# Loading two experts' down weights and the last gate's weights only after the first gathered rows, and turning the second rows between gate and up

## The reference, cut to what matters

```python
x = x + mix
x = x + hier_moe(rms_norm(x, norm2_g), ...)      # top-1 group of 4, top-2 experts of 4
x = x + sigmoid(x @ w_ple_gate) * (p @ w_ple)    # w_ple_gate is 1024 x 1024
y = rms_norm(x, final_norm_g)
# one expert e, for the rows that chose it:
act = silu(h @ w_gate[e]) * (h @ w_up[e]) * weight   # w_gate, w_up: 1024 x 256
out += act @ w_down[e]                               # w_down: 256 x 1024
```

## Time and profile before

| | us |
|---|---|
| timed runs, median of 3 | 892.86 |
| the profiled execution, own time | 888.35 |
| its span in the profile | 886.6 |
| TensorE busy | 851.8 (96%) |
| VectorE, ScalarE, GpSimd busy | 351.2, 201.5, 143.2 |
| mean granted TensorE clock | 0.991 |

### The profile page before, as it was taken

One profiled execution on the slowest core, in us unless ns is written; L12 is line 12 of the kernel. 1 busy time (PEld: TensorE's weight loads), 2 busy tenths in 40 slices (PEclk: granted clock), 3 DMA queues, 4 the chain that ended last, 5 costly groups with the idle time before them and its releaser, 6 DMA issues. The chain is left out here.

```text
span 886.6 us, 12016 instructions
## 1 busy us (share of the span) xinstructions
PE 851.8 (96%) x4227; PEld 580.2 (65%) x4227; DVE 351.2 (40%) x935; ACT 201.5 (23%) x495; POOL 143.2 (16%) x152
## 2 busy tenths in 40 slices
PE   8999999999999898989999999998999999999995
PEld 5455677777778696545677764454777777774441
DVE  3199702355542335667472451133311111114433
ACT  3010213311013164545321000231111111113121
POOL 3059002200003022345000000021111111003100
PEclk9999999999999899999999999999999999999998
DMA  9430875705113969000204292039799999965211
GB/s 334 112 102 0 187 256 154 64 1 182 40 38 93 126 186 283 9 1 1 108 1 111 81 333 76 6 124 335 251 348 368 375 362 363 359 221 190 75 48 35
DMA packets 110887, 140.47 MB, mean 158 GB/s; under 512 B 33910, under 2 KB 90298, under 8 KB 110722
## 3 DMA queue, kind: packets, MB, share of 16 engines
q1 hardware_dynamic: 93164, 110.17, 40.5%
q0 software_dynamic: 4304, 15.47, 5.2%
q10 hardware_dynamic: 13374, 14.22, 4.7%
HBM read 118.65 MB, written 23.29 MB: 160 GB/s over the span
## 5 line engine op out<-in xcount | busy, mean ns | idle before, releaser
L1062 PE MATMUL ps<-hT,w_slot 128*128 128x288 f32 x640 | 155.7, 406 | 0.2 <-ACT fin L1731 0.2
L1062 PEld LDWEIGHTS ps<-hT,w_slot 128*128 128x128 f32 x640 | 121.4, 190 | 34.3 <-issue 0.9
L1062 PE MATMUL ps<-w_slot,hT 128*128 128x512 f32 (+1 forms) x320 | 127.1, 555 | 1.9 <-DMA w_slot<-in_w_in 1.6
L1512 PE MATMUL ps<-wgu,hT 128*128 128x256 f32 x512 | 114.9, 383 | 0.7 <-DVE hT L1950 0.7
L1512 PEld LDWEIGHTS ps<-wgu,hT 128*128 128x128 f32 x512 | 98.3, 192 | 20.7 <-issue 6.7
L1062 PEld LDWEIGHTS ps<-w_slot,hT 128*128 128x128 f32 x320 | 60.0, 190 | 62.8 <-issue 42.4
L2395 DVE SCALAR_TENSOR_TENSOR th<-th,ps 128x256 f32<-128x256 f32 x16 | 6.7, 421 | 135.5 <-ACT th L1875 135.5
L1062 PE MATMUL ps<-merged,actT 128*128 128x512 f32 x128 | 58.8, 601 | 0.4 <-ACT actT L1879 0.4
L1062 PE MATMUL ps<-w_slot,merged 128*128 128x512 f32 x128 | 56.0, 594 | 1.1 <-DVE merged L1950 1.1
L1062 PEld LDWEIGHTS ps<-w_slot,merged 128*128 128x128 f32 x128 | 23.9, 190 | 29.9 <-issue 28.2
L1062 PEld LDWEIGHTS ps<-merged,actT 128*128 128x128 f32 x128 | 23.1, 189 | 24.7 <-issue 24.1
(11 more groups left out here) (402 smaller groups left out, 1153.8 us busy)
## 6 DMA issues: line engine op xcount, KB each, us to landing
wgu<-in_w_exp_gate SPq DMA_DIRECT2D x16, 1024.0 KB, 9.5
wgu<-in_w_exp_up SPq DMA_DIRECT2D x16, 1024.0 KB, 13.9
merged<-in_w_exp_down SPq DMA_DIRECT2D x16, 1024.0 KB, 12.5
w_slot<-in_w_in SPq DMA_DIRECT2D x8, 1024.0 KB, 7.3
expert_rows<-onsaT ACTq DMA_DIRECT2D x16, 512.0 KB, 6.8
hT<-gates_by_features SPq DMA_DIRECT2D x8, 576.0 KB, 3.8
w_slot<-in_w_o SPq DMA_DIRECT2D x2, 2048.0 KB, 9.1
w_slot<-in_w_ple_gate SPq DMA_DIRECT2D x2, 2048.0 KB, 24.4
```

The source lines that it names most:

```text
L1062: ins = pe.matmul(out, a, b, start=(n == 0), stop=(n == len(pairs) - 1))
L1512: ins = pe.matmul(ps[:, 2 + u, FF * w:FF * w + FF], hgT[:, u, k], wgu[:, u, w, k], start=(k == 0), stop=(k == KD - 1))
```

## The change

Two edits. SyncE waits for `hg_ld[1]`, the landing of expert 1's first gathered rows, before it issues the down weights of experts 0 and 1 and both halves of w_ple_gate. And TensorE does the turning of expert 1's rows between the gate half and the up half of gate_up(0), in place of behind gate_up(0).

```diff
             load_weights("ple")
             sp.wait_ge(pe_done, PLAN.done(("wo", NT - 2, 1)))
+            sp.wait_ge(hg_ld[1], 16)
             for u in range(2):
                 load_down(u, u)
             load_weights("pg0")
...
-            def gate_up(j, n, u, half):
+            def gate_up(j, n, u, half, between=None):
                 pe.wait_ge(gu_ld[u], j * 256 + half * 32 + 32)
                 for w in range(2):
+                    if w and between:
+                        between()
                     for k in range(KD):
...
-                gate_up(j, 0, 0, 0)
-                turn_rows(j, 1, 1, 0)
+                gate_up(j, 0, 0, 0, lambda: turn_rows(j, 1, 1, 0))
```

## The result

| | before | after |
|---|---|---|
| median of 22 timed runs of each, side by side (us) | 890.14 | 897.58 |
| fastest | 885.76 | 892.76 |
| ratio after / before, 95% interval | | 1.0085 [1.0056, 1.0113] |
| the profiled execution, span | 886.6 | 900.1 |

The change makes the kernel slower by 0.85%, some 7.6 us. The forecast was slower, by 3.85 us (0.43%): the way and the mechanism held, the size was half of what came.

A forecast was written before the change was run, and what follows sets the result against it. The prediction took TensorE to bound the expert stage, with DMA nearly as busy. Gate_up(2)'s start moves from 637.0 to 638.85, plus 2.0 us of clock: +3.85 on 892.86 gives 896.7 us, range 891.0 to 899.5.

The forecast's parts named there:

- Bound: Expert stage: TensorE is the chain, with DMA engines nearly as busy at 348 to 375 GB/s.
- The gather is freed: Ahead of gate_up(0): last store lands in 3.0 us, first gather starts 0.29 us after its list; 3.53 us halt gone.
- TensorE alone would be 6.0 us ahead at gate_up(2): Without waiting for weights, TensorE would reach gate_up(2) at 631.0 in place of 637.0.
- The backlog: Ahead of gate_up(2): SyncE released at 609.75, plus 18.4, 8.0 and 2.7 us; expert 2's weights land at 638.85.
- the worst bound: Latest landing of expert 2's weights, 641.3: release at 610, 371 GB/s ahead, 3.3 us for the rest.
- the 5 to 9 us named as a sign: Expected length of TensorE's halt ahead of gate_up(2) in the profile after, ended by the load of w_exp_up.
- the best bound: Earliest landing of expert 2's weights, 635.4: release at 608.25, all 9.96 MB at 400 GB/s, 2.2 us for the rest.
- The clock: In gate_up(2), after a halt of 7.9 us: half clock loses 2.0 us, bounds 0 and 3.
- Nothing late behind that: After gate_up(2): weight stream 1.3 us later, TensorE 3.85 later, so no second halt and the shift reaches the end.
- Bandwidth rule: Loads ahead of gate_up(2): at 358 GB/s the 7.34 MB take 20.5 us, time 898.8; prediction used 400 GB/s instead.
- The faster one: Rival, chance 0.10: expert 2's weights pass w_ple_gate at gate_up(2), TensorE keeps 6.0 us, time 886.9.
- slower by more: Rival, chance 0.13: landing at the worst bound, 641.3, or a second halt; +5.5 to +7 us, 898.4 to 900.

The follow-up runs named there:

- the kernels without the backlog: Kernel after with both halves of w_ple_gate issued behind the experts' last down load: ratio to before 0.9942 with SyncE's wait, 0.9931 without.
- nothing held: Kernel after without SyncE's wait, and with w_ple_gate's second half (pg1) issued behind the experts: ratio to before 0.9925.

## Why the prediction was right, and where its size was off

- *The number.* The absolute forecast, 896.7, lies 0.9 us from the 897.58 measured, and that is luck: it stands on a median of three runs, 892.86, where the median of 22 is 890.14. The shift is what the working gives, and it was +3.85 against some +7.5.
- *Bound.* Right: in the stretch the DMA engines are the companion of TensorE that has nothing to spare, and the loads done early had filled a stretch that is idle otherwise.
- *The gather is freed.* Right: last store 3.3 us, TensorE does not wait. The gather began 0.89 us behind its list (609.93 to 610.82), not the 0.29 I took from a gather that waited for a DMA, and its second one took 5.1 us, not 4.5. With 6.34 us of shift ahead of the stage taken off, SyncE was released at 611.06 and not 609.75: **1.3 us** too little in the sum.
- *TensorE alone would be 6.0 us ahead at gate_up(2).* Right: the kernels without the backlog have 5.96.
- *The backlog.* Right in kind; the expected 29.1 us from release to landing were 29.7: **0.6 us** too little, with 10.8 MB moved in them where the sum has 10.26. Shifted by 6.34 us, the landing is 640.8, near the worst bound, and TensorE was ready at 631.0 as forecast, so the halt was longer than the 5 to 9 us named as a sign. (The worst bound's own terms give 641.1, not 641.3, and the best bound leaves out the 0.3 MB of results that the sum has. Neither changes the reading.) With the release, gate_up(2) began 3.90 us later than before (S + 37.79 against 33.89), where I had 1.85.
- *The clock.* Right that it falls. I took 2.0 us from two halts of 2.6 and 3.5 us; the one of 9.9 cost 10.14 - 6.91 = 3.2 us, outside the bound of 3: **1.2 us** too little. The clock was already down when TensorE resumed, and stayed so longer than behind the short halts.
- *Nothing late behind that.* Right: no second halt, and the 7.1 us at gate_up(2) are the 7.2 of the stage.
- *Bandwidth rule.* The Trainium skill, page "DMA: Bandwidth & Descriptors", section Bandwidth, has transfers between HBM and SBUF bound at about 358 GB/s, and calls that figure each core's part when both cores of a domain stream; alone, its own table has a core at 425. These loads, on one core, ran at 421 in 620 to 624, with gathers beside them, and at 382 over 624 to 646. So 358 is not a ceiling here, and the prediction's contrast with it compares two cases.
- *Rivals.* The faster one needed expert 2's weights to pass w_ple_gate; they did not, and landed after 6.3 MB. Taking the bytes away step by step (4.19, 2.10, 0 MB of w_ple_gate ahead) gives halts of 9.86, 2.42 and 0 us. The same page of the Trainium skill, section "Queues, rings and completion order", has one ring's descriptors taken in order on each DMA engine. The trace agrees in the main: 8.70 MB of SyncE's queue had moved when the 8.39 up to and with expert 2's up weights had landed. In size, what came is the rival called slower by more (+5.5 to +7): its first way, a landing near the worst bound, with a clock that cost more than assumed; its other way, a second halt, did not come.

The three terms in bold, 3.1 us, with 0.1 us between the landing and the first matmul, are the difference between 3.85 and 7.1, up to rounding. Each was a duration taken from the row nearest in kind but milder than the case: a shorter halt, a quicker release. They add up in one direction because all lie on one chain.

## What to carry to other kernels

A load that is wanted late is not free to be moved later: on a queue that is taken in order, it stands ahead of everything issued behind it, and it should go where the queue is idle or behind the last load with a date. Before holding a queue, sum the bytes up to the next load that has a date, and divide by the bandwidth seen. A halt can cost more than its length, since the clock may fall in it; two halts of 2.4 us passed here without a loss, one of 2.0 and longer ones did not.

## What the runs showed of the hardware

- Halts of TensorE and the clock: behind 9.86 us idle it was at half speed up to 652 at least, 4.8 us after the restart, and 32 matmuls took 10.14 us; behind 3.53 us they took 8.79; behind 2.42 and 2.45 us, 7.17 at a full clock; yet behind 1.96 us (nothing held) a half of 16 took 5.02 in place of 3.72. The length of the halt alone does not tell.
- The clock also fell near 386 and 438 us in the kernel after, with halts of TensorE of 0.5 to 1.1 us around. The kernel before has the same halts there (0.72, 0.51 and 1.08 us from 380 to 385, 1.06 near 430) and its clock stayed at 1.00. By the estimate above, these two dips account for the 6.3 us by which that execution came late to the stage.
- The spread between timed runs goes with the clock. Of 35 runs of the kernel before that stand beside the last experiments, the 7 with a mean granted clock of 0.991 took 886.2 to 889.0 us, and the 10 with 0.982 took 893.9 to 896.5.
- An indirect gather of 0.52 MB took 4.3 and 5.1 us with the queues empty and 7.08 and 7.43 beside full ones; one of expert results took 8.8 and 9.4 beside w_ple_gate, and 4.7 in the kernel before.
- A backlog is seen in SyncE's own list: issuing expert 2's gate and up weights took 3.8 and 5.2 us in the kernel after, behind 6.3 MB, and 0.4 and 0.6 before, with a free queue.
